# Projecting the first weight slab of every stage one token block at a time, around the transposes of block 1

## The chip, the cores and the metric

The kernel runs on one core of a Trainium2 chip. The metric is the device time in microseconds; lower is better. Five engines with their own instruction queues work side by side and meet at semaphores: TensorE (matmuls and transposes), VectorE, ScalarE, GpSimd and SyncE (which issues the weight loads).

## The reference, cut to what matters

The reference is a small transformer over 256 tokens of width 1024: two layers of attention (grouped and dilated, then latent) with MLPs, and two further layers (differential attention, retention) with gated MLPs before and behind each. Nearly all of its time is in products of activations with weights in fp32. Every stage begins the same way:

```python
def rms_norm(x, g):
    xf = x.astype(jnp.float32)
    y = xf * lax.rsqrt(jnp.mean(xf * xf, axis=-1, keepdims=True) + EPS)
    return (y * g.astype(jnp.float32)).astype(x.dtype)
...
        hn = rms_norm(h, norm_mlp_g[layer])
        h = h + jnp.square(jax.nn.relu(hn @ mlp_w1[layer])) @ mlp_w2[layer]
```

The norm is over the width of each token, so it can't be finished for a token before the last product of the stage before is added to `h`.

## The kernel before, in words

**Slabs.** All weights lie in memory as 266 slabs of 128 x 2048 fp32 values (1 MB). SyncE loads them in order into a ring of six (`raw`). ScalarE casts a slab to fp32r (`whi`, L190) and VectorE subtracts to get the rest (`wlo`, L194); both are rings of three. SyncE reloads a place of the ring when `lo_ready` says that L194 has read it. TensorE uses the slabs in the same order: `slab_used` counts the ones that it is done with.

**Three products.** An fp32 product is made of three fp32r matmuls, high x high, high x low, low x high (`three`, L200 to L202). Activations are split in the same way into `xh` and `xl`, each with 8 chunks of 128 features by 256 tokens. `project_features` takes a slab's two output blocks `j` of 128 features; for each it runs 8 chunks `k` x 3 matmuls with the weights stationary and all 256 tokens moving: 48 matmuls a slab.

**Token blocks.** The 256 tokens are two blocks of 128. At the end of a stage `last_slabs` finishes block 0 of the output first, then block 1 in two halves, so that the norm of block 0 runs on VectorE and ScalarE while TensorE still works on block 1. `turn_block(pe, q, t)` transposes block `t` of the normalized activations `xn` (L302), 4 + 4 transposes into two PSUM banks, each group behind a wait for `xn_ready`. ScalarE copies a bank to `xh` (`take_high`, L325) and VectorE makes `xl` (`take_low`, L372). On both engines the work of block 0 stands in the queue ahead of the rest of the norm of block 1, and the cast and the subtraction of the stage's second slab stand behind the block 1 pieces (`norm_scalar`, `norm_vector`).

**The crossing of two stages.** There are ten norms, `q` = 0 to 9; this text calls what lies around one "crossing q". TensorE's order there is: the last products, with block 0's transposes ahead of the last piece; 12 matmuls on zeros (`stay_warm(WARM)`, L262, 512 columns of bf16, whose result nobody reads); block 1's transposes; the first slab; the second slab. `first_slabs` does the last three. Its first output block is ordered so that all products with `xh` come first (L272, L273) and those with `xl` last (L277); the second output block and the second slab are plain `project_features`.

Two crossings differ. Crossing 0 is the start of the kernel: block 0's transposes and a small table product run ahead of `first_slabs`, and there is no `last_slabs`. Crossing 4 (`FINAL_Q`) has two norms in a row, the final norm of the first half of the model and the first norm of the second half, so block 0's transposes can't stand among the last products: 12 warming matmuls stand ahead of them and 12 behind.

Of the kernel before, what the change touches and what calls it, by code (L numbers as in the profile page):

```python
# [30 lines left out]
P = 128  # L31
T = 256
TB = T // P
D = 1024
KC = D // P
# [6 lines left out]
WARM = 12  # L42
# [56 lines left out]
def program(nc, weights, x, gains, columns, consts, rel_bias, lam, scratch, out):  # L99
    with ExitStack() as ctx:  # L100
        def sb(name, shape, dt=F32):
            return ctx.enter_context(nc.sbuf_tensor(name, shape, dt))

        def sem(name):
            return ctx.enter_context(nc.semaphore(name))

        raw = sb("raw", [P, RAW, SLAB])
        whi = sb("whi", [P, SPLIT, SLAB], F32R)
        wlo = sb("wlo", [P, SPLIT, SLAB], F32R)
        h = sb("h", [P, TB, D])  # L110
        xn = sb("xn", [P, TB * D])
        xh = sb("xh", [P, KC, T], F32R)
        xl = sb("xl", [P, KC, T], F32R)
# [30 lines left out]
        up = [ctx.enter_context(nc.psum_tensor(f"up{k}", [P, 512], F32)) for k in range(4)]  # L144
# [5 lines left out]
        lo_ready = sem("lo_ready")  # L150
        slab_used = sem("slab_used")
# [18 lines left out]
        xl_ready = sem("xl_ready")  # L170
# [9 lines left out]
        def W(part, n, k, lo, hi, width=IN_W):  # L180

            return part[:, n % SPLIT, k * width + lo:k * width + hi]
# [15 lines left out]
        def three(out_ap, sh, sl, mh, ml, first, last):  # L198

            nc.tensor.matmul(out_ap, sh, mh, start=first, stop=False)  # L200
            nc.tensor.matmul(out_ap, sh, ml, start=False, stop=False)  # L201
            return nc.tensor.matmul(out_ap, sl, mh, start=False, stop=last)  # L202

        def project_features(n, bank, blocks=(0, 1)):

            for j in blocks:
                for k in range(KC):
                    mm = three(bank[:, j * T:(j + 1) * T],
                               W(whi, n, k, j * P, (j + 1) * P), W(wlo, n, k, j * P, (j + 1) * P),
                               xh[:, k, :], xl[:, k, :], k == 0, k == KC - 1)  # L210
            return mm
# [11 lines left out]
        def project_out(n, fh, fl, first=False, last=False, blocks=range(TB), halves=range(2)):  # L223

            for t in blocks:
                for k in range(OUT_K):
                    for half in halves:
                        sl = slice(half * 512, half * 512 + 512)
                        mm = three(accs[:, 2 * t + half, :],
                                   fh(k)[:, t * P:(t + 1) * P], fl(k)[:, t * P:(t + 1) * P],  # L230
                                   W(whi, n, k, sl.start, sl.stop, D),
                                   W(wlo, n, k, sl.start, sl.stop, D),
                                   first and k == 0, last and k == OUT_K - 1)
            return mm
# [3 lines left out]
        def last_slabs(pe, n, f0, f1, q, ready=None):  # L238


            pe.wait_ge(lo_ready, n + 1)
            project_out(n, *f0, blocks=(0,))
            pe.wait_ge(lo_ready, n + 2)
            if ready:
                ready()
            project_out(n + 1, *f1, last=True, blocks=(0,)).then_inc(acc_ready, 1)
            project_out(n, *f0, blocks=(1,), halves=(0,))
            project_out(n + 1, *f1, last=True, blocks=(1,), halves=(0,)).then_inc(acc_ready, 1)
            project_out(n, *f0, blocks=(1,), halves=(1,)).then_inc(slab_used, 1)
            if q is not None and q != FINAL_Q:  # L250
                turn_block(pe, q, 0)
            project_out(n + 1, *f1, last=True, blocks=(1,), halves=(1,)).then_inc(slab_used, 1)
            if q is not None:
                stay_warm(WARM)
            if q == FINAL_Q:
                turn_block(pe, q, 0)
                stay_warm(WARM)

        def stay_warm(count):

            for _ in range(count):
                nc.tensor.matmul(up[3][:, :], zero[:, 0:P], zero[:, :], start=True, stop=True)  # L262

        def first_slabs(pe, n, q):

            turn_block(pe, q, 1)
            pe.wait_ge(lo_ready, n + 1)

            for half in range(2):
                pe.wait_ge(xh_ready, 4 * q + 3 + half)  # L270
                for k in range(4 * half, 4 * half + 4):
                    nc.tensor.matmul(up[0][:, 0:T], W(whi, n, k, 0, P), xh[:, k, :], start=k == 0, stop=False)  # L272
                    nc.tensor.matmul(up[0][:, 0:T], W(wlo, n, k, 0, P), xh[:, k, :], start=False, stop=False)  # L273
            for half in range(2):
                pe.wait_ge(xl_ready, 4 * q + 3 + half)
                for k in range(4 * half, 4 * half + 4):
                    nc.tensor.matmul(up[0][:, 0:T], W(whi, n, k, 0, P), xl[:, k, :], start=False,  # L277
                                     stop=k == KC - 1)
            project_features(n, up[0], (1,)).then_inc(slab_used, 1)
            pe.wait_ge(lo_ready, n + 2)  # L280
            project_features(n + 1, up[1]).then_inc(slab_used, 1)

# [13 lines left out]
        def turn_block(pe, q, t):  # L296

            for b in (2 * t, 2 * t + 1):
                pe.wait_ge(xn_ready, 3 * q + (1 if t == 0 else b))
                for c in range(4):  # L300
                    f = t * D + (4 * (b % 2) + c) * P
                    mm = nc.tensor.transpose(up[b][:, c * P:(c + 1) * P], xn[:, f:f + P], ident)  # L302
                mm.then_inc(turned, 1)
# [162 lines left out]
        def run_feed_tensor(pe, name, kind, q, q_next):  # L466

            order, ins, per = feed(name, kind)
            first_slabs(pe, FIRST[name], q)
            zero_sums()  # L470
            turns = (len(order) - 4) // RAW
            with pe.Fori(0, turns) as i:
                for s in order[2:2 + RAW]:
                    feed_tensor(pe, name, kind, s, i, per)
            for s in order[2 + turns * RAW:-2]:
                feed_tensor(pe, name, kind, s, None, per)

            def hidden(g):
                return (lambda k: hidh[:, g % per, k, :]), (lambda k: hidl[:, g % per, k, :])

            g = order[-1][1]
            pe.wait_ge(S("feed_hidden_low"), FED[name] + g)
            last_slabs(pe, order[-2][3], hidden(g - 1), hidden(g), q_next,
                       ready=lambda: pe.wait_ge(S("feed_hidden_low"), FED[name] + g + 1))
# [333 lines left out]
        def ab_tensor(pe):  # L818
            def head_sums(j, w):
# [5 lines left out]
                mm.then_inc(S("ab_sum"), 1)  # L825

            first_slabs(pe, n_ab, 0)
            for s in range(1, 9):
                n = n_ab + s
# [137 lines left out]
        def c_tensor(pe):  # L967

            first_slabs(pe, n_c, 2)
            pe.wait_ge(S("c_sq"), 1)  # L970
            for t in range(TB):
# [317 lines left out]
        def ret_tensor(pe):  # L1289
# [23 lines left out]
            def out_(u):  # L1313
                pe.wait_ge(S("r_low"), u + 1)
                if u == RT_HEADS - 1:
                    last_slabs(pe, n_ro + 2 * u, *(features(4 * (u % 2) + 2 * s) for s in range(2)), 9)
                    return
                for s in range(2):
                    n = n_ro + 2 * u + s
                    pe.wait_ge(lo_ready, n + 1)  # L1320
                    f = features(4 * (u % 2) + 2 * s)
                    project_out(n, *f, first=(u == 0 and s == 0), blocks=(0,))
                    if s == 0:
                        sum_squares(u + 1)
                    project_out(n, *f, first=(u == 0 and s == 0), blocks=(1,)).then_inc(slab_used, 1)
                    if s == 0:
                        spread_root(u + 1)
# [94 lines left out]
        def out_tensor(pe, name, done, count, q):  # L1422

            if done[0] != "d_o_low":
                for d, c in zip(done, count):
                    pe.wait_ge(S(d), c)
            for s in range(2):
                n = FIRST[name] + s
                pe.wait_ge(lo_ready, n + 1)
                if done[0] == "d_o_low":  # L1430
                    pe.wait_ge(S("d_o_low"), s + 1)
                project_out(n, *features(2 * s), first=s == 0).then_inc(slab_used, 1)
            if done[0] == "d_o_low":
                pe.wait_ge(S("d_o_low"), 4)
            last_slabs(pe, FIRST[name] + 2, features(4), features(6), q)
# [341 lines left out]
```

## Time and profile before

| | |
|---|---|
| time, median of 3 runs | 1859.17 us (1854.91, 1859.17, 1860.91) |
| span of the profiled execution | 1854.7 us |
| the profiled execution's own time | no separate figure is shown; the fastest of the three runs is 1854.91 us |
| TensorE busy, matmuls | 1773.5 us (96%), 11839 instructions |
| TensorE busy, weight loads | 1591.5 us (86%) |
| VectorE busy | 979.0 us (53%) |
| ScalarE busy | 794.1 us (43%) |
| DMA | 291.90 MB, 157 GB/s on average |

The span goes from the first to the last instruction of one execution. Matmuls overlap each other, so a busy TensorE is not TensorE at its peak: the distance from one start to the next tells the pace. A row of the timeline can merge several instructions ("x8"); its length then runs from the first start to the last end. Some matmul records are missing from a trace, so a count may be one short.

### The profile page before, as it was taken

Reading aid. Unit: us, or ns where it says so; the run is one execution under the profiler, and the core shown is the slowest. Engines: PE = TensorE matmul, PEld = TensorE weight load, DVE = VectorE, ACT = ScalarE, POOL = GpSimd, SP = SyncE. Lnnn points to the kernel's source line nnn. Section 1 sums busy time; section 2 is a strip of 40 time slices with the busy share of each in tenths; the row PEclk is TensorE's granted clock in tenths of the full one; section 3 lists DMA queues with packets and bytes.
Section 4 is the critical chain, followed back from the end, with each engine's and each line's share of the span. In section 5 each row is a group of like instructions: output and inputs, shape, how many; then the busy total and the mean of one; then the engine's idle time right before and its main releaser. Section 6 shows DMA issues by size and latency. Waiting matters only on the chain.

```text
span 1854.7 us, 28378 instructions
## 1 busy us (share of the span) xinstructions
PE 1773.5 (96%) x11839; PEld 1591.5 (86%) x11854; DVE 979.0 (53%) x1024; ACT 794.1 (43%) x928; POOL 15.9 (1%) x39
## 2 busy tenths in 40 slices
PE   7989999979999989999987999999999999999999
PEld 6847999856899979998975899989998999879998
DVE  5565555665655555445465644454545544455444
ACT  4254444455544443334444433453334444343432
POOL 1000000010000000000000000000000000000000
PEclk8999999999999999999986999999999999999999
DMA  9303555431455634554420455545554554225450
GB/s 359 137 1 125 187 195 184 150 111 36 148 192 192 209 143 181 181 184 177 150 91 23 148 181 182 195 155 204 177 185 159 197 183 176 91 92 204 180 195 32
DMA packets 41720, 291.90 MB, mean 157 GB/s; under 512 B 4720, under 2 KB 4864, under 8 KB 7472
## 3 DMA queue, kind: packets, MB, share of 16 engines
q1 hardware_dynamic: 38880, 281.04, 42.1%
q0 software_dynamic: 2224, 8.55, 1.3%
q8 instruction: 56, 0.92, 0.2%
q10 hardware_dynamic: 544, 1.26, 0.2%
q14 instruction: 16, 0.13, 0.0%
HBM read 289.76 MB, written 1.06 MB: 157 GB/s over the span
## 4 chain that ended last, share of the span: by engine, by line
PE 87%; DVE 7%; ACT 4%; issue 2%; DMA 1%; DVEq 0%; SPq 0%; ACTq 0%
PE up L200 16%; PE up L202 16%; PE up L201 16%; PE accs L200 10%; PE accs L201 9%; PE accs L202 9%; PE accs L588 2%; PE up L302 1%; DVE mx L706 1%; PE up L567 1%; DVE xn L359 1%; DVE h L415 1%; PE accs L423 1%; ACT whi L190 1%; PE up L1340 1%
## 5 line engine op out<-in xcount | busy, mean ns | idle before, releaser
L194 DVE TENSOR_TENSOR wlo<-raw,whi 128x2048 fp32r<-128x2048 f32 x266 | 608.8, 2292 | 469.2 <-ACT whi L190 469.2
L200 PE MATMUL up<-xh,whi 128*128 128x256 f32 x2200 | 624.6, 284 | 0.0
L202 PE MATMUL up<-xh,wlo 128*128 128x256 f32 x2200 | 622.5, 283 | 0.0
L201 PE MATMUL up<-xl,whi 128*128 128x256 f32 x2200 | 622.5, 283 | 0.0
L190 ACT CAST whi<-raw 128x2048 fp32r<-128x2048 f32 x266 | 505.4, 1903 | 226.7 <-PE accs L202 159.0
L200 PEld LDWEIGHTS up<-xh,whi 128*128 128x128 f32 x2200 | 421.9, 192 | 4.5 <-issue 1.5
L201 PEld LDWEIGHTS up<-xl,whi 128*128 128x128 f32 x2200 | 422.0, 192 | 3.1 <-issue 0.5
L202 PEld LDWEIGHTS up<-xh,wlo 128*128 128x128 f32 x2200 | 422.0, 192 | 0.0
L200 PE MATMUL accs<-whi,hidh 128*128 128x512 f32 x608 | 238.3, 392 | 0.3
L201 PE MATMUL accs<-wlo,hidh 128*128 128x512 f32 x608 | 237.4, 390 | 0.0
L202 PE MATMUL accs<-whi,hidl 128*128 128x512 f32 x608 | 236.6, 389 | 0.0
L513 ACT ACTIVATE hid<-up 128x512 f32<-128x512 f32 x76 | 45.4, 597 | 270.5 <-PE up L202 270.5
L518 ACT CAST hidh<-hid 128x512 fp32r<-128x512 f32 x76 | 47.1, 620 | 206.8 <-DVE hid L534 182.4
L202 PEld LDWEIGHTS accs<-whi,hidl 128*128 128x128 f32 x608 | 114.2, 188 | 24.4
L200 PEld LDWEIGHTS accs<-whi,hidh 128*128 128x128 f32 x608 | 114.4, 188 | 23.0 <-issue 1.1
L201 PEld LDWEIGHTS accs<-wlo,hidh 128*128 128x128 f32 x608 | 114.5, 188 | 20.9
L538 DVE TENSOR_TENSOR hidl<-hid,hidh 128x512 fp32r<-128x512 f32 x76 | 52.6, 692 | 52.1 <-ACT hidh L518 52.1
L200 PE MATMUL accs<-whi,xh 128*128 128x512 f32 (+1 forms) x192 | 74.1, 386 | 4.5 <-DVE xl L1410 2.6
L202 PE MATMUL accs<-whi,xl 128*128 128x512 f32 (+1 forms) x192 | 72.1, 375 | 0.0
L201 PE MATMUL accs<-wlo,xh 128*128 128x512 f32 (+1 forms) x192 | 72.0, 375 | 0.0
L200 PE MATMUL up<-whi,xh 128*128 128x256 f32 (+1 forms) x208 | 59.2, 285 | 0.0
L201 PE MATMUL up<-wlo,xh 128*128 128x256 f32 (+1 forms) x208 | 58.7, 282 | 0.0
(211 smaller groups left out, 1725.4 us busy)
## 6 DMA issues: line engine op xcount, KB each, us to landing
raw<-weights SPq DMA_DIRECT2D x266, 1024.0 KB, 4.8
gain<-gains POOLq DMA_DIRECT2D x10, 512.0 KB, 4.0
h<-x_in SPq DMA_DIRECT2D x2, 512.0 KB, 5.8
tabs<-consts POOLq DMA_DIRECT2D x1, 1024.0 KB, 5.2
out<-h SPq DMA_DIRECT2D x2, 512.0 KB, 2.6
tabs<-consts ACTq DMA_DIRECT2D x1, 768.0 KB, 13.4
hid<-rel_scratch POOLq DMA_DIRECT2D x1, 768.0 KB, 6.9
hidh<-rel_scratch POOLq DMA_DIRECT2D x1, 768.0 KB, 8.2
```

The lines of the kernel that those rows point to most:

```text
L190: nc.scalar.copy(whi[:, m % SPLIT, :], raw[:, m % RAW, :]).then_inc(hi_ready, 1)
L194: nc.vector.tensor_tensor(wlo[:, m % SPLIT, :], raw[:, m % RAW, :], whi[:, m % SPLIT, :].bitcast(F32), ALU.subtract).then_inc(lo_ready, 1)
L200: nc.tensor.matmul(out_ap, sh, mh, start=first, stop=False)
L201: nc.tensor.matmul(out_ap, sh, ml, start=False, stop=False)
L202: return nc.tensor.matmul(out_ap, sl, mh, start=False, stop=last)
L302: mm = nc.tensor.transpose(up[b][:, c * P:(c + 1) * P], xn[:, f:f + P], ident)
L359: nc.vector.scalar_tensor_tensor(dst[:, lo:hi], h[:, t, lo:hi], rstd[:, t:t + 1], factors[:, lo:hi], ALU.mult, ALU.mult).then_inc(done, 1)
L415: nc.vector.scalar_tensor_tensor(h[:, t, lo:hi], accs[:, 2 * t + lo // 512:2 * t + hi // 512, :].rearrange("p a n -> p (a n)"), factor, h[ ...
L513: nc.scalar.activation(hid[:, g % per, :], bank[:, :], ACT.Relu if kind == "mlp" else ACT.Silu).then_inc(S("feed_act"), 1)
L518: nc.scalar.copy(hidh[:, g % per, :, :].rearrange("p a n -> p (a n)"), hid[:, g % per, :]).then_inc(S("feed_hidden_high"), 1)
L538: nc.vector.tensor_tensor(hidl[:, g % per, :, :].rearrange("p a n -> p (a n)"), hid[:, g % per, :], hidh[:, g % per, :, :].rearrange("p a ...
L588: mm = nc.tensor.matmul(a["o"](u), a["v"](u, kb), hid[:, u % 2, kb * T:(kb + 1) * T], start=kb == 0, stop=kb == TB - 1)
```

## The change

`last_slabs` no longer issues the 12 warming matmuls at a crossing; at crossing 4 all 24 now stand ahead of block 0's transposes. `first_slabs` waits for the first slab's `wlo` and for both `xl` pieces of block 0, then projects block 0 alone through both output blocks of the slab with the new `project_block` (2 x 24 matmuls with 128 tokens moving). Then come block 1's transposes, and then the first output block for block 1 in the order of before (products with `xh`, then with `xl`, 24 matmuls) and the second output block by `project_block` (24 matmuls). All of them have 128 moving columns. The second slab is as before.

```diff
--- before.py
+++ after.py
@@ -250,33 +250,42 @@
             if q is not None and q != FINAL_Q:
                 turn_block(pe, q, 0)
             project_out(n + 1, *f1, last=True, blocks=(1,), halves=(1,)).then_inc(slab_used, 1)
-            if q is not None:
-                stay_warm(WARM)
             if q == FINAL_Q:
+                stay_warm(2 * WARM)
                 turn_block(pe, q, 0)
-                stay_warm(WARM)
 
         def stay_warm(count):
 
             for _ in range(count):
                 nc.tensor.matmul(up[3][:, :], zero[:, 0:P], zero[:, :], start=True, stop=True)
 
+        def project_block(n, j, t):
+
+            for k in range(KC):
+                mm = three(up[0][:, j * T + t * P:j * T + (t + 1) * P],
+                           W(whi, n, k, j * P, (j + 1) * P), W(wlo, n, k, j * P, (j + 1) * P),
+                           xh[:, k, t * P:(t + 1) * P], xl[:, k, t * P:(t + 1) * P], k == 0, k == KC - 1)
+            return mm
+
         def first_slabs(pe, n, q):
 
+            pe.wait_ge(lo_ready, n + 1)
+            pe.wait_ge(xl_ready, 4 * q + 2)
+            for j in range(2):
+                project_block(n, j, 0)
             turn_block(pe, q, 1)
-            pe.wait_ge(lo_ready, n + 1)
-
+
+            late = up[0][:, P:T]
             for half in range(2):
                 pe.wait_ge(xh_ready, 4 * q + 3 + half)
                 for k in range(4 * half, 4 * half + 4):
-                    nc.tensor.matmul(up[0][:, 0:T], W(whi, n, k, 0, P), xh[:, k, :], start=k == 0, stop=False)
-                    nc.tensor.matmul(up[0][:, 0:T], W(wlo, n, k, 0, P), xh[:, k, :], start=False, stop=False)
+                    nc.tensor.matmul(late, W(whi, n, k, 0, P), xh[:, k, P:T], start=k == 0, stop=False)
+                    nc.tensor.matmul(late, W(wlo, n, k, 0, P), xh[:, k, P:T], start=False, stop=False)
             for half in range(2):
                 pe.wait_ge(xl_ready, 4 * q + 3 + half)
                 for k in range(4 * half, 4 * half + 4):
-                    nc.tensor.matmul(up[0][:, 0:T], W(whi, n, k, 0, P), xl[:, k, :], start=False,
-                                     stop=k == KC - 1)
-            project_features(n, up[0], (1,)).then_inc(slab_used, 1)
+                    nc.tensor.matmul(late, W(whi, n, k, 0, P), xl[:, k, P:T], start=False, stop=k == KC - 1)
+            project_block(n, 1, 1).then_inc(slab_used, 1)
             pe.wait_ge(lo_ready, n + 2)
             project_features(n + 1, up[1]).then_inc(slab_used, 1)
```

## Rows read from the trace of the kernel before

**Rows 1.** The profile page: span, granted clock by slice, chain of work by engine.

```profile
span 1854.7 us, 28378 instructions
...
PEclk8999999999999999999986999999999999999999
...
PE 87%; DVE 7%; ACT 4%; issue 2%; DMA 1%; DVEq 0%; SPq 0%; ACTq 0%
```

**Rows 2.** The view of waits, TensorE: us in total, times, longest.

```profile
PE up L302 <- DVE xn L359: 19.0, 19, 6.0
```

**Rows 3.** Timeline of crossing 2: start, us taken, engine, line, operation, [idle before].

```profile
354.90 1.29 DVE L372 TENSOR_TENSOR xl<-up,xh 128x512 fp32r<-128x512 f32 x2 [0.77 <-ACT xh L325]
...
356.15 2.54 PE L262 MATMUL up<-zero 128*128 128x512 bf16 x11
...
359.00 1.32 PE L302 MATMUL up<-mats,xn 128*128 128x128 f32 x8 [0.31 <-DVE xn L359]
...
359.69 1.25 ACT L325 CAST xh<-up 128x512 fp32r<-128x512 f32 x2 [1.80 <-PE up L302]
...
360.42 0.36 PE L272 MATMUL up<-xh,whi 128*128 128x256 f32 x1
...
360.83 3.71 ACT L190 CAST whi<-raw 128x2048 fp32r<-128x2048 f32 x2
...
362.78 4.49 DVE L194 TENSOR_TENSOR wlo<-raw,whi 128x2048 fp32r<-128x2048 f32 x2 [1.11 <-ACT whi L190]
```

**Rows 4.** Windows row (length, busy (count) by engine, clock); next slab's first matmul.

```profile
360.41:366.24 5.83, 5.82 (x48) 5.83 (x49) 4.71 (x4) 4.14 (x3) 0.00 (x0) 1.00 0.06 7
...
366.25 0.28 PE L200 MATMUL up<-xh,whi 128*128 128x256 f32 x1
```

**Rows 5.** Forty-eight matmuls with 128 moving columns: second, last, windows row.

```profile
53.69 0.28 PE L201 MATMUL up<-wlo,xh 128*128 128x128 f32 x1
...
58.83 0.28 PE L202 MATMUL up<-whi,xl 128*128 128x128 f32 x1
...
53.70:58.93 5.23, 5.23 (x49) 5.23 (x49) 2.02 (x3) 0.00 (x0) 0.00 (x0) 1.00 0.55 171
```

**Rows 6.** Timelines of crossings 1 and 9: block 0's low part, second slab.

```profile
167.71 1.29 DVE L372 TENSOR_TENSOR xl<-up,xh 128x512 fp32r<-128x512 f32 x2 [0.77 <-ACT xh L325]
...
179.28 0.28 PE L200 MATMUL up<-xh,whi 128*128 128x256 f32 x1
...
1657.55 1.29 DVE L372 TENSOR_TENSOR xl<-up,xh 128x512 fp32r<-128x512 f32 x2 [0.77 <-ACT xh L325]
...
1668.88 0.28 PE L200 MATMUL up<-xh,whi 128*128 128x256 f32 x1
```

**Rows 7.** Crossing 0: timeline rows and one windows row.

```profile
15.94 1.28 DVE L372 TENSOR_TENSOR xl<-up,xh 128x512 fp32r<-128x512 f32 x2
...
18.78 1.97 PE L302 MATMUL up<-mats,xn 128*128 128x128 f32 x8 [2.40 <-DVE xn L359]
...
22.00:24.00 2.00, 2.00 (x12) 2.00 (x11) 0.89 (x2) 2.00 (x2) 0.00 (x0) 0.55 1.03 430
...
27.87 0.28 PE L200 MATMUL up<-xh,whi 128*128 128x256 f32 x1
```

**Rows 8.** Crossing 4 (final normalization): timeline rows, one windows row, second slab.

```profile
659.47 2.54 PE L262 MATMUL up<-zero 128*128 128x512 bf16 x11
...
661.84 1.04 PE L302 MATMUL up<-mats,xn 128*128 128x128 f32 x8
...
663.10 1.29 DVE L372 TENSOR_TENSOR xl<-up,xh 128x512 fp32r<-128x512 f32 x2 [0.94 <-ACT xh L325]
...
669.97 1.97 PE L302 MATMUL up<-mats,xn 128*128 128x128 f32 x8 [4.50 <-DVE xn L359]
...
669.90:675.50 5.60, 5.53 (x25) 5.25 (x26) 3.17 (x5) 4.11 (x4) 0.53 (x1) 0.50 0.30 94
...
679.40 0.28 PE L200 MATMUL up<-xh,whi 128*128 128x256 f32 x1
```

## The prediction

> **What bounds the kernel now.** I read the page first: TensorE holds 87% of the chain that ended last, DMA 1%, and the granted clock is full in nearly every slice [rows 1]. So what counts is time on TensorE's own queue. The view of waits says where that queue stands idle: the largest entry is the block transposes (L302), 19.0 us in 19 waits for the scaled activations `xn` [rows 2]. They stand at the stage crossings, where the change acts, so I read one crossing as a timeline, number 2, and laid the others beside it.
>
> In crossing 2 [rows 3] the low half of token block 0 (L372, two pieces) is done at 354.90 + 1.29 = 356.19. TensorE runs the warming matmuls from 356.15 to 358.7 (12 in the code; one record is missing). The transposes of block 1 start at 359.00, released by VectorE's `xn`, which needs nothing of TensorE. The first projection matmul starts 1.42 us behind them, at 360.42: four transposes and one ScalarE copy lie between. The slab then takes to 366.25: 48 matmuls of 256 moving columns in 5.83 us, 0.120 us each [rows 4]. From block 0 being complete to the second slab it is 366.25 - 356.19 = 10.06 us. That is the stretch to beat.
>
> **What the change costs and gives.** It removes 12 warming matmuls; they fill a time in which TensorE would wait for block 1 anyway, so this gives nothing by itself. It replaces 48 matmuls of 256 columns by 96 of 128: 48 for block 0 as soon as its `xl` is there, 48 for block 1 behind the transposes. Everything hangs on the price of a matmul with 128 columns.
>
> The trace has 48 of them in a row with the same shapes (128x128 stationary, 128 moving) in the fifth slab of the first stage: from the second at 53.69 to the last at 58.83 are 46 steps, 0.1116 us each, at a granted clock of 1.00 [rows 5]. Against 0.120 for 256 columns, halving the columns saves 7% of a matmul, not half. Weight loads are busy for the whole 5.23 us of that stretch, and every matmul brings its own load of 128 columns; I take it that the load sets the pace. So each half of the slab costs 48 x 0.1116 = 5.36 us.
>
> The new crossing 2, in order: block 0 complete at 356.19, plus 0.11 from a semaphore to the first matmul (as from ScalarE's first copy, 359.69 + 0.62, to L272 at 360.42 in rows 3) = 356.30; plus 5.36 = 361.66, where the transposes can start. They were ready to go at 359.00, so the early part overshoots by 2.66 us. Plus 1.42 = 363.08, plus 5.36 = 368.44, against 366.25: **+2.19 us**. Put otherwise: 96 x 0.1116 - 5.83 = 4.88 us of added TensorE work, of which the 2.70 us from 356.30 to 359.00 are hidden.
>
> The other crossings at full clock repeat this. In crossing 9 block 0 is complete at 1657.55 + 1.29 = 1658.84; plus 0.11 + 5.36 + 1.42 + 5.36 = 1671.09, against 1668.88: +2.21. Crossing 1: 167.71 + 1.29 + 12.25 = 181.25, against 179.28: +1.97 [rows 6]. Seven are like 2 and 9 (2, 3, 5, 6, 7, 8, 9): 7 x 2.20 + 1.97 = **17.4 us**.
>
> Queued behind the moved transposes are ScalarE's `xh` copies of block 1 and then its casts (L190); VectorE's `xl` of block 1 and then L194, which makes `wlo`; and SyncE's loads, which wait for L194. In crossing 2 the first of the two L194 ends at 362.78 + 2.25 = 365.03, 6.03 us behind the start of the transposes [rows 3]; the second slab will be wanted 1.42 + 5.36 = 6.78 behind it. So it is in time by some 0.7 us and no new wait forms; were it late, each crossing would pay the excess. The gain load on GpSimd waits for `xn` alone and doesn't move. The loads run up to six slabs ahead, so 2 us more cost them nothing.
>
> **Crossing 0** is at half clock (1.2 GHz) before: TensorE works without a break from 18.78, and a clock of 0.55 over 22 to 24 puts the rise to full at 23.8 [rows 7]. Block 0 is complete at 17.22. No row has a 128-column projection at half clock; the nearest are the 128-column transposes, 8 in 1.97 us with a last duration of 0.48, so 0.213 each [rows 7]. If the clock rises as long after steady work begins as before, 5.0 us, it does so at 22.3: 23.3 matmuls by then, 24.7 x 0.1116 = 2.8 more, 25.1; plus 1.42 + 5.36 = 31.8 against 27.87: **+3.9**. Bounds: full clock at once gives 17.33 + 5.36 + 6.78 = 29.5, +1.6; rising at 23.8 as before gives +4.7.
>
> **Crossing 4** follows two norms in a row, and the 12 warming matmuls that stood behind block 0's transposes now stand ahead of them. Before, the first 12 run right up to the transposes at 661.84, whose row shows no idle time [rows 8]. Twelve more, at 2.54 us with the tail for eleven, hold them back some 2.56 us; VectorE and ScalarE finish block 0 before the rest of block 1's norm, so block 1 is late by the same, 669.97 becomes 672.53. The early projection runs from 663.10 + 1.29 + 2.56 + 0.11 = 667.1 to 672.4 and is just covered. What comes back is clock: before, TensorE stood idle for 4.50 us ahead of 669.97 and then worked at 0.50 over 669.9 to 675.5 [rows 8]; now it is quiet for 1.6 us. With full clock the second slab is due at 672.53 + 6.78 = 679.31, against 679.40: **-0.1**. If the clock falls nonetheless and takes as many matmuls as before (25 in those 5.6 us, 0.10 more each), +2.5.
>
> **Sum.** 17.4 + 3.9 - 0.1 = +21.2 us, 1.1% of the profiled span of 1854.7. That execution lies at the low edge of the three times; the median is 4.5 above its span, and I add the same time to it: 1859.2 + 21.2 = **1880 us**. The bounds give +18.9 (17.4 + 1.6 - 0.1) to +24.6 (17.4 + 4.7 + 2.5), which is 1878 to 1884 on the median; with the 6 us that the three runs lie apart, mostly downward, and a little for what is not seen, 1872 to 1889.
>
> **The rule that speaks against this.** The Trainium skill (TensorE: Matmul & The Clock Gate, section Back-to-back issue gap) gives a sustained stream of weight loads and matmuls some 81 ns for each at 128 moving columns. By that figure the second slab of crossing 2 would start 0.8 us earlier than before and the whole sum would be about -7 us: 1852 us, an estimate from that page. The trace disagrees: its 48 matmuls took 0.1116 us each with these fp32r operands.
>
> **Rivals.**
> *Narrow matmuls cheaper than in rows 5* (faster). Crossing 2 breaks even at 96p + 1.42 = 366.25 - 356.30, so p = 0.0889 us; below it the change gains. For it: the same `whi` block is stationary twice in a row here, in rows 5 it is `xh`. Against: the 256-column form also repeats its block and still has weight loads busy for all of 5.83 us [rows 4]. At the extreme, half of 0.120, the second slab starts at 359.18 + 1.42 + 2.88 = 363.48, 2.8 earlier, and all ten crossings give about -25: 1834 us. Chance 0.04.
> *The delay is given back later in the stage* (no change). It takes a later TensorE wait for work that TensorE did not release; what speaks against it is that DMA is 1% of the chain [rows 1] and that the slab chain above moves with the transposes. 1862 us; chance 0.05. Within 0.3% is about what a measurement of this kernel can tell from no change.
> *The clock falls at the crossings*, narrow matmuls counting for less (slower still). One half slab at 0.213 is 4.9 us more in each of 8 crossings: 1880 + 39 = 1919. Against: 1.00 granted over the narrow ones of rows 5, and TensorE idles less than before. Chance 0.05.
> *The forecast as worked out:* 0.86. A sliver of its low side falls within 0.3%, so faster 0.04, same 0.06, slower 0.90.
>
> **What the profile after would show.** Right, if: matmuls of 128 columns stand 0.11 us apart; block 1's transposes no longer wait for `xn` and start 5.4 to 5.5 us behind the end of block 0's L372; the second slab starts 12.2 us behind that end where it was 10.06; L194 of the second slab is done before TensorE asks; crossing 4 stays at full clock with its transposes 2.6 us later. Wrong, if the pace is under 0.09, if the transposes still wait for `xn`, or if later waits shrink by what the crossings add.

## The result, and the profile after

The change made the kernel slower: 1895.99 us (median of 4 runs, 1888.16 to 1897.85) against 1857.2 us, ratio 1.0202, 95% interval 1.0182 to 1.0222. The forecast was 1880 with a range of 1872 to 1889; the direction was right, the time lies above the range, and the added time was 38.8 us where 21.2 were forecast. The profiled execution is the fastest of the four, 1888.16 us with a span of 1886.4.

From the page of the kernel after, the lines that answer to rows 1:

```profile
span 1886.4 us, 29154 instructions
...
PEclk6989999989999999999997999999999999999999
...
PE 88%; DVE 6%; ACT 4%; issue 1%; DMA 1%; SPq 0%; DVEq 0%; ACTq 0%
```

TensorE holds one per cent more of the chain. The clock line tells where to look: its first digits are 6, 9, 8 where they were 8, 9, 9 [rows 1], and each slice is 47 us.

**Crossing 2** in the timeline of the kernel after (L381 is what was L372, L311 was L302, L334 was L325):

```profile
371.95 1.29 DVE L381 TENSOR_TENSOR xl<-up,xh 128x512 fp32r<-128x512 f32 x2 [0.77 <-ACT xh L334]
...
373.39 0.30 PE L200 MATMUL up<-xh,whi 128*128 128x128 f32 x1 [0.26 <-DVE xl L381]
...
378.66 0.28 PE L202 MATMUL up<-xh,wlo 128*128 128x128 f32 x1
...
378.78 1.06 PE L311 MATMUL up<-mats,xn 128*128 128x128 f32 x8
...
379.44 1.07 ACT L334 CAST xh<-up 128x512 fp32r<-128x512 f32 x2 [4.50 <-PE up L311]
...
380.07 0.33 PE L282 MATMUL up<-xh,whi 128*128 128x128 f32 x1 [0.24 <-ACT xh L334]
...
380.39 3.72 ACT L190 CAST whi<-raw 128x2048 fp32r<-128x2048 f32 x2
...
382.34 4.49 DVE L194 TENSOR_TENSOR wlo<-raw,whi 128x2048 fp32r<-128x2048 f32 x2 [1.00 <-ACT whi L190]
...
385.49 0.33 PE L200 MATMUL up<-xh,whi 128*128 128x256 f32 x1
```

Nearly every step stands where the forecast put it. Block 0 is complete at 371.95 + 1.29 = 373.24. The narrow matmuls run from 373.39 to 378.66, 47 steps of 0.112 us. The transposes follow at 378.78, 5.5 us behind the end of L381, and wait for no `xn`. Over the whole kernel the waits of rows 2 went from 19.0 us in 19 to 9.9 in 9; what is left is 6.5 at the start and some 0.4 ahead of block 0's transposes at eight crossings:

```profile
PE up L311 <- DVE xn L368: 9.9, 9, 6.5
```

The late part starts 1.29 us behind them (1.42 forecast), and the second slab starts at 385.49, 12.25 us behind block 0's `xl` where it was 10.06 [rows 3, 4]. The first L194 ends at 382.34 + 2.25 = 384.6, 0.9 us before TensorE asks: no new wait. Measured from block 0's first transpose to the second slab, crossings 2, 3 and 5 to 9 are each 2.18 to 2.20 us longer than before and crossing 1 is 1.96 us longer, 17.3 us together; the forecast was 17.4.

**Crossing 4**, timeline, and a windows row (length, busy time and count of TensorE, weight loads, VectorE, ScalarE, GpSimd, then the granted clock) of the same kernel:

```profile
688.96 1.04 PE L311 MATMUL up<-mats,xn 128*128 128x128 f32 x8
...
697.09 1.32 PE L311 MATMUL up<-mats,xn 128*128 128x128 f32 x8
...
703.84 0.34 PE L200 MATMUL up<-xh,whi 128*128 128x256 f32 x1
```

```profile
691.70:703.80 12.10, 12.08 (x104) 11.57 (x105) 8.06 (x13) 8.62 (x13) 0.53 (x1) 1.00 0.14 45
```

The clock is full where it was 0.50 [rows 8]. From crossing 3's second slab to this one is 195.11 us, before 195.18: -0.07, forecast -0.1.

**Crossing 0** is where it went wrong. Timeline rows, first the first and last of the early matmuls, then the second slab; below, windows of the same kernel:

```profile
17.40 0.45 PE L200 MATMUL up<-xh,whi 128*128 128x128 f32 x1 [1.13 <-DVE xl L381]
...
27.46 0.41 PE L202 MATMUL up<-xh,wlo 128*128 128x128 f32 x1
...
39.73 0.52 PE L200 MATMUL up<-xh,whi 128*128 128x256 f32 x1
```

```profile
17.40:27.60 10.20, 10.20 (x48) 10.20 (x48) 1.58 (x3) 0.29 (x1) 0.00 (x0) 0.50 1.01 420
29.40:39.70 10.30, 10.30 (x49) 10.28 (x49) 6.46 (x5) 4.19 (x3) 0.53 (x1) 0.50 0.42 135
39.70:42.80 3.10, 3.10 (x16) 3.10 (x16) 0.42 (x1) 2.38 (x2) 2.04 (x3) 0.50 0.85 343
42.80:50.00 7.20, 6.61 (x64) 6.35 (x63) 2.50 (x3) 2.06 (x2) 0.00 (x0) 1.00 0.99 382
```

The granted clock is 0.50 through both narrow parts and the transposes between them, at 0.214 us a matmul, and rises only at 42.8, 3.1 us after the wide matmuls of the second slab began. Before, it rose at 23.8 [rows 7], and the first wide projection matmul had begun at 20.66. These are that matmul and the windows row from it to the rise, in the kernel before:

```profile
20.66 0.55 PE L272 MATMUL up<-xh,whi 128*128 128x256 f32 x1
...
20.66:23.80 3.14, 3.14 (x16) 3.14 (x16) 1.86 (x3) 3.02 (x3) 0.00 (x0) 0.50 1.01 423
```

The second slab starts at 39.73 where it was 27.87: +11.9 us, where 3.9 were forecast and 4.7 was the upper bound.

**The sum of this execution:** 11.9 (crossing 0) + 17.3 (eight crossings) - 0.1 (crossing 4) = 29.1 of the 31.7 us by which the span grew. The remaining 2.6 lie between crossings. In the stage behind crossing 0, up to crossing 1, 3.2 us were added, some 1.5 of them by its second slab's 3.1 us at half clock. Ahead of crossing 3, 3.1 were added; ahead of crossing 6, 3.7 were gained. All three hold attention. The other three executions were 6 to 10 us longer than this one, with a mean clock of 0.968 or 0.969 where this one has 0.973; no trace of them is on record.

### The profile page after: what moved, and what is told of

It reads as the page before. It is cut to its first block, busy times and chain, and to the rows that moved or that the text cites. A ratio compares the mean times of both kernels' runs of the same rounds, so it can differ in the third digit from the quotient of the medians.

```text
span 1886.4 us, 29154 instructions
## 1 busy us (share of the span) xinstructions
PE 1808.8 (96%) x12231; PEld 1639.6 (87%) x12238; DVE 978.0 (52%) x1024; ACT 793.2 (42%) x928; POOL 15.9 (1%) x39
## 4 chain that ended last, share of the span: by engine, by line
PE 88%; DVE 6%; ACT 4%; issue 1%; DMA 1%; SPq 0%; DVEq 0%; ACTq 0%
PE up L200 17%; PE up L202 17%; PE up L201 17%; PE accs L200 9%; PE accs L201 9%; PE accs L202 9%; PE accs L597 2%; DVE mx L715 1%; PE up L576 1%; ACT whi L190 1%; PE accs L432 1%; PE up L1349 1%; DVE wlo L194 1%; DVE xl L381 1%; PE up L311 1%
## 5 line engine op out<-in xcount | busy, mean ns | idle before, releaser
L194 DVE TENSOR_TENSOR wlo<-raw,whi 128x2048 fp32r<-128x2048 f32 x266 | 608.8, 2292 | 469.2 <-ACT whi L190 469.2
L200 PE MATMUL up<-xh,whi 128*128 128x256 f32 (+1 forms) x2360 | 672.7, 285 | 4.9 <-DVE xl L381 4.9
L201 PE MATMUL up<-xl,whi 128*128 128x256 f32 (+1 forms) x2360 | 669.7, 284 | 0.0
L202 PE MATMUL up<-xh,wlo 128*128 128x256 f32 (+1 forms) x2360 | 669.7, 284 | 0.0
L200 PEld LDWEIGHTS up<-xh,whi 128*128 128x128 f32 x2360 | 456.5, 193 | 14.5 <-issue 11.6
L201 PEld LDWEIGHTS up<-xl,whi 128*128 128x128 f32 x2360 | 456.6, 193 | 3.1 <-issue 0.5
L202 PEld LDWEIGHTS up<-xh,wlo 128*128 128x128 f32 x2360 | 456.5, 193 | 0.0
```

What stands on the lines that cost most here:

```text
L194: nc.vector.tensor_tensor(wlo[:, m % SPLIT, :], raw[:, m % RAW, :], whi[:, m % SPLIT, :].bitcast(F32), ALU.subtract).then_inc(lo_ready, 1)
```

## The experiments

In all diffs below, `first_slabs_wide` is `first_slabs` of before and `first_slabs_narrow` that of the change. All times compare with runs of the kernel before on the same chip. Theory A is that narrow matmuls leave a low clock low; theory B that crossing 0's long low stretch was chance. A profile is that of one execution; a time is the median over all of them.

### The change at crossing 0 alone

```diff
+        def first_slabs(pe, n, q):
+            (first_slabs_narrow if q == 0 else first_slabs_wide)(pe, n, q)
```

The warming matmuls at the crossings are those of before.

> The new first_slabs at crossing 0 alone, everything else as before. Theory A (matmuls of 128 columns don't lift the granted clock once it is low, so crossing 0 runs at half clock until wide matmuls come): half clock until about 42 us from the start, second slab 11 to 12 us later than before, and the whole kernel 13 to 16 us slower. Rival B (the long half-clock stretch after the change was chance, the forecast's +3.9 us holds): full clock by 24 us, kernel 2 to 5 us slower.

Measured: 1870.46 us against 1856.11, +14.4 us, ratio 1.0072 (1.0049 to 1.0096). Windows of this kernel:

```profile
17.40:40.00 22.60, 22.33 (x105) 22.14 (x105) 8.23 (x10) 5.07 (x5) 0.53 (x1) 0.50 0.64 258
40.00:43.10 3.10, 3.10 (x16) 3.10 (x17) 0.45 (x1) 2.38 (x2) 2.05 (x3) 0.50 0.99 352
43.10:50.00 6.90, 6.30 (x61) 6.05 (x61) 2.20 (x3) 1.85 (x2) 0.00 (x0) 1.00 1.00 387
```

The same picture as in the full change, to a tenth of a microsecond: half clock until 43.1, 3.1 us into the second slab, which starts at 40.0. It isn't chance: in all five profiles with this crossing 0 (the first, this one and three further down) the clock is 0.50 from 17.4 to 39.7 us, the second slab starts at 39.7 to 40.0, and the clock rises at 42.4 to 44.1. B falls. That the width of the matmuls is the cause, as theory A has it, is for the next experiments to show.

### The change at all crossings but 0

```diff
+        def first_slabs(pe, n, q):
+            (first_slabs_narrow if q != 0 else first_slabs_wide)(pe, n, q)
```

The warming matmuls at the crossings are gone, as in the full change.

> The change at every crossing but 0. Theory A: 17 to 18 us slower than before (seven crossings at +2.2, one at +2.0, crossing 4 at about -0.1), which is 14 to 20 us faster than the full change. Rival B: the excess sits in these crossings or behind them, and the kernel is 28 us or more slower than before.

Measured: 1874.33 us, +18.2, ratio 1.0094 (1.007 to 1.0118). The forecast for these nine crossings was 17.4 - 0.1. This half of the sum was right. With crossing 0 alone it makes 32.6 us. The full change was measured three times, at +38.8, +37.1 and +33.1 us (the last two stand further down), so 6.2, 4.5 or 0.5 us are in neither part. The ratios are 1.0202, 1.022 and 1.0182 where the two parts add up to 1.0166; with intervals of 0.002 or more on each of them, an excess over the parts is likely but not certain.

### The full change with the clock brought up first

```diff
-            stay_warm(WARM)
+            stay_warm(40)
             pe.wait_ge(mats_loaded, 16)
             turn_block(pe, 0, 0)
             table_tensor(pe)
+            stay_warm(12)
```

> The full change, with 40 warming matmuls of 512 columns ahead of block 0's transposes at the start in place of 12, and 12 more behind the table product. Theory A: the clock is full when the narrow matmuls of crossing 0 begin and they don't let it fall, so the second slab starts at about 29 to 30 us and the kernel is 11 to 16 us faster than the full change, some 19 us slower than before. If narrow matmuls also pull a full clock down, the clock falls during crossing 0 and little is gained.

Measured: 1879.77 us, +23.7, ratio 1.0109 (1.007 to 1.0147), so 9 to 15 us less than the three measurements of the full change. The expected +19 was 5 us too low: crossing 0 (+1.7), the eight crossings (+17.3) and crossing 4 make 18.9 in this trace, and the largest of the differences between the crossings is +4.7 in the stage with the first attention. One windows row from 17 us to the second slab:

```profile
17.00:29.50 12.50, 12.13 (x106) 11.62 (x105) 6.33 (x10) 4.97 (x5) 0.00 (x0) 1.00 0.87 360
```

The clock is full before the narrow matmuls begin and stays full; the second slab starts at 29.5. So narrow matmuls held a high clock here, where they did not bring back a low one in the runs above.

### Crossing 0 alone, with wide work ahead of the narrow

```diff
             table_tensor(pe)
+            stay_warm(18)
```

> The new first_slabs at crossing 0 alone, with 18 warming matmuls of 512 columns put behind the table product, ahead of the narrow ones: 7 us of added work at half clock. Theory A (narrow matmuls don't lift a low clock, wide ones do): full clock by 20 to 24 us, second slab at 33 to 36 us instead of 40, kernel 4 to 7 us faster than with crossing 0 alone. Rival: the clock is low for another reason, the added work delays the second slab to 44 us or more.

Measured: 1866.2 us, +9.7, ratio 1.004 (1.0025 to 1.0055); 4.7 us less than the +14.4 of crossing 0 alone. Windows of this kernel:

```profile
16.00:22.00 6.00, 6.00 (x15) 1.97 (x15) 2.91 (x7) 0.87 (x3) 0.00 (x0) 0.50 1.01 423
22.00:35.00 13.00, 12.76 (x109) 12.02 (x108) 4.31 (x5) 4.67 (x4) 0.00 (x0) 1.00 0.45 187
```

The clock is full from 22 us. TensorE did 18 matmuls more and its second slab starts at 35.1 where it was 40.0. Work was added on the bounding engine, and even the slowest of the ten executions (1868.42) is faster than the fastest of the four without it (1869.12). The windows show why: the same narrow matmuls run behind wide ones at 1.00 instead of 0.50. The profile is that slowest execution; it gains 4.9 us in crossing 0 and loses 4.2 of them again further on.

Together with the first two, this leaves theory A. The matmuls of the second slab have the data type of the narrow ones and differ from them in their columns, and the clock rose while they ran; the warming matmuls differ in data type too. Whether narrow ones would raise the clock if they went on for longer than 22 us, no run shows.

### The kernel before without warming

```diff
-            if q is not None:
+            if q == FINAL_Q:
                 stay_warm(WARM)
-            if q == FINAL_Q:
                 turn_block(pe, q, 0)
                 stay_warm(WARM)
```

> The kernel before without the 12 warming matmuls at crossings 1, 2, 3, 5, 6, 7, 8 and 9 (crossing 4 as before), first slab as before. If warming gives nothing there, as the prediction has it: within 2 us of before. Rival: TensorE is then quiet for 3.1 us ahead of block 1's transposes, the clock falls in some of the eight crossings at about 3 us each, and the kernel is 5 to 25 us slower.

Measured: 1866.42 us, +10.3, ratio 1.0049 (1.0036 to 1.0061). The windows row of crossing 2 in this kernel, then two of the kernel before: its crossing 2, and its first attention stage, which is for further down:

```profile
354.00:369.20 15.20, 12.11 (x70) 11.22 (x71) 10.14 (x13) 7.48 (x11) 0.00 (x0) 0.78 0.10 32
```

```profile
353.60:366.20 12.60, 12.11 (x81) 9.61 (x83) 8.86 (x12) 7.49 (x11) 0.00 (x0) 1.00 0.01 2
85.40:142.40 57.00, 46.65 (x200) 27.06 (x200) 37.13 (x110) 26.24 (x86) 0.00 (x0) 0.94 0.04 16
```

0.78 against 1.00, and 15.1 us from block 0's transposes to the second slab instead of 12.7. In this profile the clock falls in each of the eight crossings but the first. So "this gives nothing by itself", as the prediction said of the removed matmuls, was half the truth: by themselves they are worth 10 us. The change could drop them only because its narrow matmuls, which started with the clock full, keep it there (1.00 in crossings 1 to 9 of the profile after).

### Only what fits into the gap, early

```diff
-            for j in range(2):
-                project_block(n, j, 0)
+            project_block(n, 0, 0)
...
-            project_block(n, 1, 1).then_inc(slab_used, 1)
+            project_features(n, up[0], (1,)).then_inc(slab_used, 1)
```

Crossing 0 is as before.

> Crossing 0 as before; at the others only the first output block of the slab is projected early for block 0 (24 narrow matmuls, 2.68 us, as long as the gap), then the transposes, 24 narrow ones for block 1 and the second output block wide as before. If the overshoot of the early part was the cost and the narrow matmuls hold the clock: second slab 0.2 to 0.3 us earlier than before in eight crossings, kernel 0 to 4 us faster than before. Rival: 24 narrow matmuls don't hold the clock where 12 wide warming ones did, it falls in several crossings as without warming, and the kernel is 5 to 12 us slower than before.

Measured: 1857.78 us against 1856.47, ratio 1.0007 (0.9997 to 1.0018). Eight crossings take 0.27 us less each from block 0's transposes to the second slab (12.4 where crossing 2 took 12.7), as expected, and the clock stays full there. The kernel as a whole is not measurably faster (0 to 4 us faster were expected). Crossing 4 gives the gain back, in its windows row:

```profile
660.00:683.20 23.20, 19.21 (x107) 16.68 (x105) 12.38 (x17) 10.44 (x17) 0.53 (x1) 0.71 0.22 78
```

0.71: half an early part ends sooner, TensorE is quiet for longer ahead of the last transposes, and the second slab comes 4.7 us later against crossing 3 than before. The crossings thus add 2.5 us, while this profile's span is 4.1 us shorter than that of before: its third and fourth attention stages had less time at half clock. A single profile's span is not the median.

### More wide warming, nothing else

```diff
             if q == FINAL_Q:
                 turn_block(pe, q, 0)
-                stay_warm(WARM)
+                stay_warm(32)
...
-            stay_warm(WARM)
+            stay_warm(40)
...
             table_tensor(pe)
+            stay_warm(18)
```

> The kernel before with more warming: 40 in place of 12 at the start, 18 behind the table product, 32 in place of 12 behind block 0's transposes of crossing 4. If wide work keeps the clock up: crossings 0 and 4 at full clock, second slabs at 26.0 us (was 27.9) and about 2 us earlier in crossing 4, kernel 3 to 5 us faster than before. Rival: the attention stages' low stretches move with the start and take it back; then within 2 us of before.

Measured: 1851.79 us, -4.7, ratio 0.997 (0.9958 to 0.9982). Crossings 0 and 4 are at full clock, the second slab of crossing 0 starts at 26.2, and crossing 4's comes 2.2 us earlier against crossing 3:

```profile
12.00:26.10 14.10, 13.50 (x86) 9.27 (x85) 10.42 (x13) 9.10 (x12) 0.24 (x1) 1.00 1.01 420
...
667.00:682.70 15.70, 15.40 (x100) 10.77 (x98) 10.74 (x17) 10.46 (x17) 0.53 (x1) 1.00 0.13 38
```

### The full change again

> The full change once more, beside the parts. If the parts add up (crossing 0 alone +14, the other crossings +18): 30 to 34 us slower than before. Rival: the parts interact, the later start of each attention stage finds more time at half clock, and it is 37 us or more slower, as the first measurement had it.

Measured: 1893.56 us (six runs, 1889.9 to 1917.73), ratio 1.022 (1.0177 to 1.0264): +37.1, the rival's number. The slowest of the six, 1917.73, had a mean clock of 0.952, the others 0.967 to 0.972. This profile's span is 37.9 us longer than that of before. Crossing 0 again gives 11.9 and the others 17.3, but from crossing 0's second slab to crossing 1's it adds 12.4, 2.0 of them in crossing 1 itself. The first attention stage, from its first bias product (L939 before) to its last transposes of probabilities, in the profile first measured and in this one:

```profile
98.70:157.50 58.80, 48.53 (x200) 27.94 (x200) 37.11 (x110) 26.24 (x86) 0.00 (x0) 0.91 0.04 15
```

```profile
98.50:164.70 66.20, 56.05 (x200) 31.35 (x200) 37.33 (x110) 26.25 (x86) 0.00 (x0) 0.79 0.03 14
```

The same 200 TensorE instructions took 57.0 us at a clock of 0.94 before, 58.8 at 0.91, and 66.2 at 0.79. TensorE works there in short pieces behind VectorE and ScalarE. The half-clock stretches in it add up to 27 us in this profile, to 10 in the one first measured and to 6.8 us before.

### Does the moment at which the attention stage starts matter?

```diff
             first_slabs(pe, n_ab, 0)
+            stay_warm(8)
```

> The kernel before with 8 wide warming matmuls (1.7 us of TensorE time at full clock) behind the second slab, at 34 us; crossing 0 itself unchanged. It only starts all that follows later. Theory C (the clock falls in the first attention stage for longer when that stage starts at another moment against the clock's own changes): first attention stage 5 to 10 us longer at half clock than the 6.8 us of before, kernel 4 to 8 us slower. Rival D (the longer half clock there comes from what crossing 0 did to the clock): 6.8 us at half clock as before, kernel 1.7 us slower.

> The same with 16 warming matmuls, 3.4 us. Theory C: the moment counts and not the amount, so twice the delay may cost less than once; if the stage falls well again, half clock in the first attention stage is back at about 7 us and the kernel is 3 to 4 us slower. Rival D: 3.4 us slower. If both delays lengthen the half clock, it is the delay as such.

Measured: 1861.56 us for 8 (+5.5, ratio 1.0022, 1.0011 to 1.0034) and 1860.18 us for 16 (+4.1, ratio 1.0022, 1.001 to 1.0033). The attention stage of the one and then of the other:

```profile
87.40:153.60 66.20, 56.09 (x200) 31.40 (x200) 37.30 (x110) 26.28 (x86) 0.00 (x0) 0.79 0.03 13
```

```profile
88.60:148.60 60.00, 49.67 (x200) 28.42 (x200) 37.21 (x111) 26.29 (x86) 0.00 (x0) 0.89 0.04 16
```

With crossing 0 untouched and 1.7 us of delay, the stage takes 66.2 us at 0.79 in this profile, as in the full change run again; with 3.4 us of delay 60.0 at 0.89. So the longer half clock does not need a disturbed crossing 0, and rival D falls. That the delay brought it about is not shown. The profile of the single delay is the slowest of its twelve executions (its span is 10.9 us longer than that of before, the median only 5.5), and by the intervals the single delay costs 2.0 to 6.3 us and the double one 1.9 to 6.1, so beyond the 1.7 and 3.4 us of added work little is left for the one and possibly nothing for the other.

Two other profiles show what happens without any shift. The kernel with the change at all crossings but 0 and, further down, the one with the parts that gained run the same code up to crossing 1, that of the kernel before, and both reach the stage at 85.8 us. This is the stage of the one and then of the other:

```profile
85.80:142.90 57.10, 46.80 (x200) 27.25 (x200) 37.13 (x110) 26.21 (x86) 0.00 (x0) 0.94 0.04 16
```

```profile
85.80:146.70 60.90, 51.37 (x200) 29.58 (x200) 37.19 (x110) 26.20 (x86) 0.00 (x0) 0.86 0.04 15
```

So the clock of this stage differs from one execution to the next, and theory C is neither refuted nor shown. The executions of the kernel before differ too: they ran from 1852.71 us at a mean clock of 0.978 to 1862.67 at 0.970.

### A delay on top of the full change

The same line in the full change, and the full change beside it on the same chip.

> The full change with 8 wide warming matmuls, 1.7 us, behind the second slab of the first stage. Theory C (the first attention stage loses to the clock according to the moment at which it starts): the added work moves the stage away from where the full change put it, half clock inside it falls from the 10 to 27 us of the two profiles of the full change to some 7 to 10, and the kernel is 0 to 8 us faster than the full change beside it. Rival: the delay simply adds, 1.7 us or more slower than the full change.

> The full change, on the same chip as the kernel beside it: 1.020 to 1.022 of before, half clock in the first attention stage over 10 us.

Measured: 1892.99 us with the delay, ratio 1.0174 (1.0154 to 1.0194), and 1892.21 without, ratio 1.0182 (1.0158 to 1.0205). The attention stage of the one and then of the other:

```profile
101.00:162.60 61.60, 51.31 (x200) 29.24 (x200) 37.22 (x110) 26.27 (x86) 0.00 (x0) 0.86 0.03 14
```

```profile
99.10:159.90 60.80, 51.47 (x200) 29.42 (x200) 37.35 (x111) 26.36 (x86) 0.00 (x0) 0.86 0.04 15
```

Both are at 0.86, with 17 us at half clock; 7 to 10 were expected with the delay. The medians are 0.8 us apart, too little to tell a gain from a cost of 1.7 us, so the forecast of a better moment was a miss and this pair tells nothing between the two. The third measurement of the full change, 1.0182, also lies below the 1.020 to 1.022 that was expected of it.

What can be said goes by kernels whose code is the same up to crossing 1. Five profiles have that of the kernel before: four had 6.8 us at half clock in this stretch and one 17. Four have that of the full change: 10, 10, 17 and 27 us. In the seven with another start or a delay it was 14 to 27. So the change may lengthen it, but one code alone spreads by 10 to 17 us, and what decides between them stays open.

### The parts that gained, together

The half-sized early part at crossings 1 to 3 and 5 to 9, the wide slab with 32 warming matmuls at crossing 4, and crossing 0 as before:

```diff
+            (first_slabs_narrow if q not in (0, FINAL_Q) else first_slabs_wide)(pe, n, q)
```

> Crossing 0 as before; at 1 to 3 and 5 to 9 no warming and 24 narrow matmuls of block 0 ahead of block 1's transposes, the second output block wide; crossing 4 with the wide first slab and 32 warming matmuls behind block 0's transposes in place of 12. Gains to add: 8 times 0.27 us and some 2.2 us at crossing 4, where the clock stays full: 3 to 6 us faster than before. Rival: the shifts move the attention stages against the clock and take it back, within 2 us of before.

Measured: 1850.66 us against 1856.11, ratio 0.9965 (0.9952 to 0.9978), -5.5, within what was expected (3 to 6). With the warm start as well:

> The same with more warming at the start as well (40 in place of 12, and 18 behind the table product): crossing 0 at full clock, second slab 1.7 us earlier than before. Sum: 5 to 8 us faster than before, 2 to 3 us faster than the kernel before with more warming alone. Rival: the first attention stage has more time at half clock, as it had when only the warming was added, and it is no faster than the version that leaves crossing 0 alone.

Measured: 1848.79 us, ratio 0.9951 (0.9933 to 0.9969), -7.3. It beats both kernels. Its crossings 0 and 4:

```profile
12.00:26.20 14.20, 13.30 (x86) 9.20 (x84) 10.43 (x13) 9.18 (x12) 0.17 (x1) 1.00 1.01 420
667.00:682.70 15.70, 15.35 (x98) 10.73 (x98) 10.73 (x17) 10.46 (x17) 0.53 (x1) 1.00 0.10 34
```

Both are at 1.00. Its first attention stage had 20.5 us at half clock (17.1 in the profile of the version without the warm start), so what the rival named was there too; by the medians the start still gained 1.8 us on the version without it, within what the two intervals leave open.

## Why the prediction was right in sign and too small in size

*The pace.* 0.1116 us for 128 columns: measured 0.112 at full clock and 0.214 at half. Right, and with it the main point, that halving the columns saves next to nothing, so that 4.9 us of work are added to hide 2.7. The figure of the Trainium skill that spoke against it (TensorE: Matmul & The Clock Gate, section Back-to-back issue gap, 81 ns) was not seen in these fp32r matmuls. The prediction took it that the weight load sets the pace; no run here separates the load from the matmul.

*Eight crossings at full clock.* 17.4 forecast, 17.3 in the trace, 18.2 us for all but crossing 0 in time. Right. Block 1's transposes lost their wait, L194 was in time. Here the mechanism was right, not only the number.

*Crossing 4.* -0.1 forecast, -0.07 in the trace, for the reasons given: transposes later, clock full.

*Crossing 0.* This is the step that failed: "If the clock rises as long after steady work begins as before, 5.0 us, it does so at 22.3", with "rising at 23.8 as before" as the far bound. It supposed that any steady work does the same, and counted the 5.0 us from 18.78, where transposes of 128 columns began; the wide matmuls began at 20.66. In the new kernel the clock rose at 42.8, after 96 narrow matmuls had run at half clock and 3.1 us of wide ones. The term was 3.9 and measured 11.9 at the second slab; alone, this crossing made the kernel 14.4 us slower. The rival about narrow matmuls and the clock was there, but it was put at the eight crossings with a full clock, where it did not come true (1.00 throughout), and not at the one crossing with a low clock, where it did. The Trainium skill (TensorE: Matmul & The Clock Gate, section Why this matters for your kernels) advises to keep TensorE busy without a break to get the full clock; the trace disagrees for this stretch, in which TensorE was busy for the whole of 10.2 and then of 10.3 us at 0.50.

*The stages between.* The sum took everything between the crossings as unchanged. The first attention stage was not: its clock was 0.94 before and 0.91, 0.79 and 0.86 in the three profiles of the full change. In the traces the crossings give 29.1 us; the three medians are 4.0 to 9.7 us above that, and the stages between are where the rest lies. A part of it can be the luck of the executions, since this stage was at 0.94 and at 0.86 in two profiles with the same code up to its end; whether the change adds to it, and how, stays open. With the crossings alone, 1857.2 + 29.1 = 1886.3 us would have lain inside the range, by its added width and not because crossing 0 was understood: its 8.0 us of error would have been covered by luck.

*The warming.* That its removal "gives nothing by itself" was right for this change only. The price of taking the matmuls away, 10 us, should have stood beside it, and with it the condition that the narrow matmuls hold the clock.

## What to carry to other kernels

Before work is cut into narrower pieces to fill a gap, take the pace of the narrow form from a row: here two halves cost 10.75 us against 5.83, 1.84 times the whole, and in the trace what fits into the gap (24 matmuls) gained 0.27 us a crossing where twice as many lost 2.2. Price such a step separately where the granted clock is low, since the work that holds a high clock may not bring a low one back. And where a stage runs in short pieces and not at full clock throughout, its time can differ by 9 us from one profile to the next with the same instructions, so compare medians of many runs and look at the granted clock of that stage before giving a small difference a cause.

## What the runs showed of the hardware

- At 0.50 granted clock, TensorE busy without a gap on matmuls of 128 moving columns did not get the full clock for 10.2 us and again for 10.3 us, with eight transposes between; it came while matmuls of 256 columns ran, at 42.4 to 44.1 us in five profiles. With 18 bf16 matmuls of 512 columns ahead of them it was full by 22 us. With the clock at 1.00 when the narrow ones began, it stayed there over the 12.5 us of crossing 0 and in crossings 1 to 9.
- Twelve such wide matmuls, 2.5 us of TensorE time, in each of eight gaps of 3 us are worth 10.3 us in this kernel.
- From one start to the next, an fp32r matmul with 128 moving columns took 0.112 us at full clock and 0.214 at half, one with 256 columns 0.120 us at full clock and, at half, no more than the narrow one (sixteen stand in 3.10 us).
- The same 200 TensorE instructions of an attention stage took 57.0 us at a mean clock of 0.94 and 66.2 at 0.79, in profiles of kernels that do the same work there.
